# A router's logits with the 16 router columns held in TensorE and the tokens streamed, in a two-layer trunk with a mixture of experts

## What is computed

```python
scores = sigmoid(t @ w_router)                 # (512, 1024) @ (1024, 16)
biased = (scores + b_router).reshape(-1, 4, 4)
group_score = top_k(biased, 2)[0].sum(-1)      # the best group of four
best_group = argmax(group_score, -1)
...
_, idx = top_k(masked, 2)                      # the two best in that group
wts = take_along_axis(scores, idx, -1)
wts = wts / wts.sum(-1, keepdims=True)
for e in range(16):
    hid = silu(t @ w_gate[e]) * (t @ w_up[e])
    out = out + gates[:, e:e + 1] * (hid @ w_down[e])
```

## Time and profile before

| what | value |
|---|---|
| median of 3 runs | 713.5 us (708.53, 713.5, 719.13) |
| the profiled execution | 712.45 us |
| its span in the trace | 710.7 us |
| TensorE busy | 654.4 us (92% of the span) |
| VectorE busy | 356.5 us (50%) |
| ScalarE busy | 176.8 us (25%) |
| mean granted TensorE clock | 0.962 |

### The profile page before, as it was taken

How to read it: one execution, slowest core, us unless ns; L and a number is a source line. 1 busy time by engine, 2 the same in 40 slices (tenths; PEclk the granted TensorE clock), 3 DMA queues, 4 the chain that set the end, 5 groups by cost and what they waited for, 6 DMA issues and landing times. The chain is left out here.

```text
span 710.7 us, 8088 instructions
## 1 busy us (share of the span) xinstructions
PE 654.4 (92%) x2831; PEld 341.0 (48%) x2831; DVE 356.5 (50%) x712; ACT 176.8 (25%) x454; POOL 92.9 (13%) x80
## 2 busy tenths in 40 slices
PE   4899989999899898799999999779879999999975
PEld 3455434444344474455555545258645545554532
DVE  4126698897984335853422322156686323232215
ACT  5101222333332421212122222134321212222113
POOL 0010000000000022112312212100011222212210
PEclk9999999999999996999999999999899999999997
DMA  9999987976998314759999997285574989999726
GB/s 329 360 368 364 373 304 257 392 268 227 322 332 326 155 62 147 294 202 331 316 348 380 369 365 274 50 364 205 202 288 192 341 304 355 381 373 375 284 49 237
DMA packets 54542, 203.76 MB, mean 287 GB/s; under 512 B 7933, under 2 KB 17209, under 8 KB 42212
## 3 DMA queue, kind: packets, MB, share of 16 engines
q1 hardware_dynamic: 45012, 183.62, 68.0%
q0 software_dynamic: 8912, 18.85, 10.6%
q10 hardware_dynamic: 576, 0.76, 0.3%
HBM read 189.94 MB, written 23.11 MB: 300 GB/s over the span
## 5 line engine op out<-in xcount | busy, mean ns | idle before, releaser
L1788 PE MATMUL ps<-ring,work 128*128 128x512 f32 x288 | 130.8, 607 | 0.2 <-DMA ring<-in_w_up_dram 0.2
L906 DVE SCALAR_TENSOR_TENSOR acc<-adaw,cond,acc 128x1024 f32<-128x1024 f32 x70 | 89.8, 1283 | 9.7 <-DMA adaw<-in_w_ada_dram 7.6
L1788 PEld LDWEIGHTS ps<-ring,work 128*128 128x128 f32 x288 | 55.2, 194 | 69.2 <-issue 69.2
L1612 PE MATMUL psY<-xu,ring 128*128 128x512 f32 x192 | 87.3, 608 | 0.0
L814 ACT ACTIVATE work<-ps 128x256 f32<-128x256 f32 (+1 forms) x32 | 11.0, 344 | 234.4 <-PE ps L1788 172.4
L1328 DVE TENSOR_TENSOR work<-work,ps 128x256 f32<-128x256 f32 (+1 forms) x32 | 11.8, 370 | 107.1 <-ACT work L814 86.8
L1827 PE MATMUL psY<-ring,work 128*128 128x512 f32 x144 | 65.2, 595 | 0.0
L1612 PEld LDWEIGHTS psY<-xu,ring 128*128 128x128 f32 x192 | 36.1, 193 | 47.2 <-issue 47.0
L1357 DVE SCALAR_TENSOR_TENSOR work<-psY,work,gbc 128x512 f32<-128x512 f32 x40 | 28.2, 746 | 59.6 <-DMA h_dram<-work 35.5
L584 POOL DMA_INDIRECT h_dram<-work x20 | 32.7, 1637 | 164.7 <-DMA h_dram<-work 67.1
L807 ACT ACTIVATE work<-psA,modc,scl 128x128 f32<-128x128 f32 (+1 forms) x120 | 42.6, 436 | 46.7 <-PE psA L1767 44.4
(11 more groups left out here) (244 smaller groups left out, 822.0 us busy)
## 6 DMA issues: line engine op xcount, KB each, us to landing
adaw<-in_w_ada_dram SPq DMA_DIRECT2D x84, 512.0 KB, 5.6
ring<-in_w_gate_dram SPq DMA_DIRECT2D x24, 1024.0 KB
ring<-in_w_up_dram SPq DMA_DIRECT2D x24, 1024.0 KB
ring<-in_w_down_dram SPq DMA_DIRECT2D x24, 1024.0 KB, 16.0
xu<-in_w_gate_dram SPq DMA_DIRECT2D x8, 1024.0 KB
xu<-in_w_up_dram SPq DMA_DIRECT2D x8, 1024.0 KB
xu<-in_w_down_dram SPq DMA_DIRECT2D x8, 1024.0 KB
work<-in_w_ada_dram SPq DMA_DIRECT2D x12, 512.0 KB, 9.9
```

The costliest lines, as they stand in the source:

```text
L906: dve.scalar_tensor_tensor(total, adaw[:, n % ABUF, :], cond[:, k:k + 1], total if k else brow[:, :], ALU.mult, ALU.add).then_inc(mac_step, 1)
L1612: ins = pe.matmul(bank, wt, uT[:, k, :], start=(k == 0), stop=(k == KD - 1))
L1788: ins = pe.matmul(gu_ps[j % 2][:, :].rearrange("p (a f) -> p a f", a=2), xgT[:, j % 2, k, :], w_gu(j % 4)[:, :, k, :], start=(k == 0), sto ...
```

## The change

The roles in the router's matmul are exchanged. `wr[:, k, :]`, 16 columns, is held, and tokens of `uT` are streamed, so the logits stand on 16 partitions with the tokens along the free dimension. In layer 0 the three first tiles are one block of 384 columns in ps5 (`logits(1, 0, 3)`), tile 3 goes to psA; in layer 1 it is still a tile per call. ScalarE takes two sigmoids on 16 rows, one over 384 tokens as soon as three tiles are counted and one over the last 128, into `sigT`, which lies in `hid`. TensorE's new `turn_sig` turns the four pieces back into the 64 columns of ps2 where the logits used to be. VectorE waits for that, adds the bias straight from ps2, and then copies the scores from ps2 to `sig_tile`, which the gates need later. `turn_sig` stands ahead of keep_clock(3).

```diff
+        sigT = hid.rearrange("p b f -> p (b f)")[0:E, :]
...
-                act.wait_ge(logits_ready, T * (l + 1))
-                act.activation(sig_tile, ps2[:, 0:T * E], ACT.Sigmoid).then_inc(sig_ready, 1)
+                act.wait_ge(logits_ready, T * (l + 1) - 1)
+                act.activation(sigT[:, 0:3 * P], ps5[0:E, 0:3 * P], ACT.Sigmoid).then_inc(sig_ready, 1)
+                act.wait_ge(logits_ready, T * (l + 1))
+                act.activation(sigT[:, 3 * P:SEQ], psA[0:E, 0:P], ACT.Sigmoid).then_inc(sig_ready, 1)
                 expert_loop(l)
...
-                dve.wait_ge(sig_ready, l + 1)
+                dve.wait_ge(sig_turned, l + 1)
...
                 link(dve.tensor_tensor(bia.rearrange("p (t e) -> p t e", t=T),
-                                       sig_tile.rearrange("p (t e) -> p t e", t=T),
+                                       ps2[:, 0:T * E].rearrange("p (t e) -> p t e", t=T),
                                        brb[:, :].unsqueeze(1).broadcast_to([P, T, E]), ALU.add))
 
+                dve.tensor_copy(sig_tile, ps2[:, 0:T * E])
...
-            def logits(s, t):
+            def logits(s, t, tiles=1):
...
-                done = (1 + s // 2) * T + t + 1
+                done = (1 + s // 2) * T + t + tiles
                 pe.wait_ge(uT_act, done)
                 pe.wait_ge(uT_dve, done)
+                toks = slice(t * P, (t + tiles) * P)
+                dst = psA[0:E, 0:P] if t == T - 1 else ps5[0:E, toks]
                 for k in range(KD):
-                    ins = pe.matmul(ps2[:, t * E:(t + 1) * E], uT[:, k, t * P:(t + 1) * P], wr[:, k, :],
-                                    start=(k == 0), stop=(k == KD - 1))
-                ins.then_inc(logits_ready, 1)
+                    ins = pe.matmul(dst, wr[:, k, :], uT[:, k, toks], start=(k == 0), stop=(k == KD - 1))
+                ins.then_inc(logits_ready, tiles)
+
+            def turn_sig(l):
+
+                for t in range(T):
+                    if t in (0, T - 1):
+                        pe.wait_ge(sig_ready, 2 * l + (2 if t else 1))
+                    ins = pe.transpose(ps2[:, t * E:(t + 1) * E], sigT[:, t * P:(t + 1) * P], ident[0:E, 0:E])
+                ins.then_inc(sig_turned, 1)
...
             def route(l):
 
+                turn_sig(l)
                 keep_clock(3)
...
-                    for t in range(3):
-                        logits(1, t)
+                    logits(1, 0, 3)
                     turn_tile(1, 3)
                     logits(1, 3)
```

More of the change, by code:

```diff
@@ L284, in trunk @@
         logits_ready, sig_ready = sem("logits_ready"), sem("sig_ready")
+        sig_turned = sem("sig_turned")
         cstb_ready = sem("cstb_ready")
```

## The result

The change makes the kernel faster by about half a per cent: 708.33 us median (704.43 to 711.19, 20 runs) against 713.52 (708.43 to 719.13, 20 runs), a ratio of 0.994 with a 95% interval from 0.9914 to 0.9965. In a later set of runs the same kernel stood at 0.9911 (0.9877 to 0.9945). Medians and ranges take in all executions; a ratio leaves out those more than 1.5% above the fastest of their kernel. The forecast was 710.6, in a range from 706 to 717, which is a gain of 1.9 us on the profiled execution's 712.45. The measured gain is 5.2 us.

A forecast was written before the change was run, and what follows sets the result against it. Experts run at TensorE's pace; VectorE's first add, behind the router's logits, sets when they start. 712.45 - 3.3 (layer 0) + 0.6 (layer 1) = 709.75, plus 0.8 for the clock: 710.6 us, range 706 to 717.

The forecast's parts named there:

- Layer 0: Router to VectorE's first add in layer 0: the add comes earlier, -3.3 us in sum, mostly through the full clock.
- the block: Layer 0's logits of tiles 0 to 2: 16 records of 384 columns take 5.16 us instead of 6.55.
- the copy: VectorE's copy of the scores to sig_tile behind the add, each layer: adds 0.15 us, between nothing and 0.25.
- The turn back: Four new f32 transposes on TensorE after the sigmoids, each layer: the last is exposed, 0.45 us, between 0.42 and 0.67.
- The 384-wide block alone gives 1.4 of it: Layer 0, tiles 0 to 2: of 3.9 us saved up to tile 3's logits, the block's width gives 1.4.
- Layer 1: Layer 1's router: logits unchanged at the full clock; second sigmoid, turn back and copy are exposed, +0.6 us.
- The saving passes whole: Gathers and weight loads behind the routing shift with VectorE's add, so the whole saving reaches the end.
- The allowance for the clock further on: Behind the routing, lower TensorE clock costs +0.4 us per layer, between nothing and 0.9; 0.8 in the sum.
- rival A: Behind layer 0's routing, an exposed turn and most of expert 0's product run at low clock: 2.8 us lost, 712.5; chance 0.20.
- B: Layer 0's logits: 16 held columns don't hold the clock, it falls as before; slower, 714.0 us; chance 0.17.
- C: Clock holds throughout and expert 1's product loses nothing in either layer, 1.9 us each: 706.0 us; chance 0.08.
- D: Router's logits: narrow f32 held block doesn't stream as two passes, each record could double: about 719 us; chance 0.05.

The follow-up runs named there:

- later set: The whole change, both one-layer kernels and the wide stream run again side by side against the kernel before; the whole change measured 0.9911, 706.82 us.
- three-tile kernel: The whole change, but layer 0's tiles 0 to 2 as three calls of 128 columns instead of one block of 384: 0.9953, 708.97 us.
- layer-0 kernels: New form in layer 0 only, against before; flaw: layer 1's sigmoid table load stands behind the logits wait. 0.9993, 712.98 us; again 0.995, 710.17 us.
- layer-1 kernels: New form in layer 1 only, against before; flaw: layer 0's sigmoid table load stands behind the logits wait. 1.0043, 715.0 us; again 1.0006, 714.01 us.
- keep_clock(5): The whole change with keep_clock(5) instead of keep_clock(3) ahead of the positions: 0.9928, 707.9 us.
- wide-stream kernel: Kernel before, tokens still held, but 128 columns streamed against them instead of 16: 0.9907, 706.58 us; again 0.9919, 706.73 us.

## Why the prediction was right, and where it was off

**The number.** 708.33 us lies near 710.6 and well inside the range, but the range was made wide for the scatter of single executions. The forecast gain, 712.45 - 710.6 = 1.9 us, is little more than a third of the 5.2 measured, and counted from the median of 713.5 instead of the profiled 712.45 the same terms give 711.6, 3.3 us above what was measured. The medians also resolve far less than the 14 us that I took for the limit; the interval is 0.3% to either side, about 2 us.

**Layer 0: right, nearly to the tenth.** The forecast put the add 10.48 us behind the start of the logits (270.08 - 259.60); it is 10.51 (266.68 - 256.17), and 10.50 to 10.58 in each kernel with the new form and nothing else altered in front of it. Of its terms the block was 5.16 against 5.27 from start to start, tile 3's logits 1.86 against 1.91, the wide sigmoid 0.50 against 0.48, the narrow one 0.28 against 0.27, the copy 0.15 against 0.14. The turn back was the term without a row: 0.45, and 0.32 from the sigmoid's end to the add, under the lower bound of 0.42 that I had. That the sum is right to 0.03 us is in part luck: from the turn of tile 3 to its logits it took 0.11 us more than forecast (264.15 - 261.44 = 2.71 against 267.45 - 264.85 = 2.60), and the sigmoid and the turn back took 0.14 less.

**One split of it was wrong.** "The 384-wide block alone gives 1.4 of it" is not so. The working had the refutation in it: 48 thin records at 0.107 us are 5.1 us, as much as the block. The three-tile kernel shows the width to be worth 0.07 us. All but that of layer 0's gain is the clock.

**Layer 1: the step that failed** is "the logits go tile by tile between turns, at the full clock already: 16 records of 0.107 give way to 16 of 0.1075, nothing ... +0.6 us". For the profiled execution it is right (9.64 to 10.17, and the copy). But that execution was a lucky one. In three of the five traces with the old form the clock falls within layer 1's logits, and then the change takes 3.9 to 4.4 us off the distance (14.57 - 10.17 = 4.4) where I had it add 0.5. The sign of the layer's term was thus taken from one execution. The row that should have warned me stood in the prediction: the clock fell at the end of 505 to 506, straight behind the thin records, and in layer 0 within them. A fall a little earlier had to be reckoned with.

**What it adds up to.** Averages over the five traces per layer give 14.1 us in layer 0 (13.91, 13.57, 14.09, 14.3, 14.8) and 12.6 in layer 1 with the old form. With 10.5 and 10.2 for the new one, that is -3.6 and -2.4. The copy adds 0.15 in layer 0, and behind layer 1's add 1.1 us are given back, the copy's share included: about -4.8 us. The runs measured 713.52 - 708.33 = 5.2, and 713.07 - 706.82 = 6.3 in the later set. The step "The saving passes whole" is thus not borne out for layer 1. The layers' own shares by run time stay rough: less 1.3 us for the flaw, the two layer-0 kernels stand 1.8 and 4.2 us under the 713.5 and 713.1 of before, the two layer-1 kernels 0.2 us above and 0.4 below, where the distances ask for 3.6 and 2.4. With intervals of 1.6 to 3 us on each side this agrees with the distance in layer 0. In layer 1 the intervals end at 2.3 and 2.0, just short of 2.4, and take in the 1.3 that are left of it at the end of the span. That the fall in layer 1 comes in three of five executions is itself counted on five traces.

**The allowance for the clock further on.** I had added 0.4 us a layer. From the add to the gate table it was 26.17 and 26.09 us before, and 26.83, 26.24, 26.14 and 26.22 in the two later traces; after, 26.56 and 26.39, in the second trace 26.42 and 26.09. That is 0.1 more on average, which the copy is enough to explain. The falls behind the routing come as before, and after the change the clock reads 1.00 from 277 to 294, where rival A had expert 0's product at the low clock. keep_clock(5) moves a fall, and its trace is no shorter for it (27.10 and 26.35). Rival A is thus ruled out in the traces up to the gate table, and the allowance of 0.8 in the sum had nothing to stand for there.

**The rivals.** B, that 16 held columns don't hold the clock, is refuted: 1.00 over 256 to 262 and over 492 to 499. C had a gain of 6 us, close to what was measured, but by another way, expert 1's product. That takes 8.78 and 8.54 us, where it took 8.81 in both layers before: 0.3 us, not 3.8. D is refuted by the starts, 0.33 us apart.

The rule that the Trainium skill states for the clock ("TensorE: Matmul & The Clock Gate", HAM oscillation), idle gaps between bursts, does not account for these falls. The trace disagrees with it as far as it means gaps between instructions: in the second trace of before the clock falls at the end of 496 to 501, with TensorE busy 4.98 of 5.00 us, and is low over 502 to 511 with 9.00 of 9.00. Whether the array idles inside a thin record the profile can't tell.

## What to carry to other kernels

In this kernel f32 matmuls that streamed 16 columns against 128 held ones left TensorE "busy" by the profile, and its clock fell all the same; 128 columns streamed in nearly the same time, wanted or not, went with a clock of 1.00 in every trace. Where a profile shows such a fall under thin matmuls, a wider stream is worth a try. Where the granted clock changes near a stage, one profiled execution tells which side it fell on that time: take several traces before a term of a sum is read from it, and compare distances within a trace, not spans. And before a gain is ascribed to a wider tile, multiply the old records out at the full clock.

## What the runs showed of the hardware that I had not expected

Within a chain of f32 matmuls back to back, without a pause on TensorE, the clock fell from 1.00 to 0.50 in every trace with the thin logits in layer 0 (five of five). It never fell within the logits with 128 or 384 columns streamed, whether 128 or 16 were held (nine traces of each layer).

The copy of constants on VectorE (f32 to bf16, SBUF to SBUF, 128x128) takes 0.25 us alone and waits out a memset on POOL. POOL's memset after the change (its copy, at 263.92, is shown above), and then the copy and the memset of the kernel before in its second trace:

```profile
262.42 3.53 POOL L567 MEMSET work<- 128x4096 f32 x1
```

```profile
266.71 0.51 DVE L1116 CAST work<-cst 128x128 bf16<-128x128 f32 x1
...
263.57 3.53 POOL L565 MEMSET work<- 128x4096 f32 x1
```

In both the copy ends 0.12 us behind the memset (266.07 and 265.95; 267.22 and 267.10), whenever it began. Moved behind the wait, it begins when the memset is over and takes 0.26:

```profile
267.56 0.26 DVE L1121 CAST work<-cst 128x128 bf16<-128x128 f32 x1 [2.68 <-PE ps L1592]
267.70 0.22 DVE L1124 TENSOR_TENSOR work<-ps,brb 128x64 f32<-128x64 f32 x1
```

That is what the Trainium skill has ("SBUF — State Buffer", Who interferes with whom): one pair of ports is shared by VectorE and GpSimd; where a VectorE copy uses both of its ports, whichever of the two engines issued first holds the pair for its whole instruction, and the other waits in full. The trace agrees, 2.15 against 0.25 us; that this copy uses both ports no run here shows. Here the change had moved the copy into the memset by making everything in front of it faster; it ended 0.6 us before it would have been on the path. In the wide-stream kernel it was 2.27 us long and ended 0.27 us ahead of the add.
